# Decay differences in a chunked state-space scan: from mask products on TensorE to broadcast rows of running sums

## What is computed

```python
acum = jnp.cumsum(dt * a_neg.reshape(G, R), axis=2)
seg = acum[:, :, :, None] - acum[:, :, None, :]
decay = jnp.exp(jnp.where(causal[:, :, None, None], seg, -jnp.inf))
cb = jnp.einsum('bclgn,bcsgn->bclsg', Cm, Bm)
wts = cb[..., None] * decay * dt[:, :, None]
y_diag = jnp.einsum('bclsgr,bcsgrp->bclgrp', wts, x)
```

## Time and profile before

| | |
|---|---|
| median of the runs | 1535.14 us (1532.01 to 1537.67) |
| the profiled execution, its own time | 1531.77 us |
| its span in the trace | 1530.0 us |
| granted TensorE clock, mean | 0.949 of full |
| TensorE busy | 1419.6 us, 93% of the span |
| VectorE busy | 554.8 us, 36% |
| ScalarE busy | 389.2 us, 25% |
| POOL busy | 441.1 us, 29% |

### The profile page before, as it was taken

The page is one execution under the profiler, slowest core; times in us unless marked ns, Lnnn a source line. Parts: engine busy times, 40 slices in busy tenths (PEclk is TensorE's granted clock), DMA queues, the critical chain, the costliest instruction groups (busy, mean ns, idle before and its releaser), DMA issues.

```text
span 1530.0 us, 24111 instructions
## 1 busy us (share of the span) xinstructions
PE 1419.6 (93%) x9214; PEld 1217.3 (80%) x9214; DVE 554.8 (36%) x798; ACT 389.2 (25%) x581; POOL 441.1 (29%) x382
## 2 busy tenths in 40 slices
PE   6999999999998999999899799999789999999990
PEld 6999999997687769768876799954778788878870
DVE  3344420055457547546653511111521111111115
ACT  5211134443234234233323411101211101111112
POOL 5244433344235324433532433300010100010002
PEclk8999999999999989999999899999689999999995
DMA  5233222252044025106203222366149999999925
GB/s 135 56 82 76 77 70 78 82 139 56 1 135 105 14 64 148 42 0 161 78 14 89 56 82 74 118 226 284 47 155 341 344 327 344 344 337 337 343 91 199
DMA packets 179226, 220.04 MB, mean 144 GB/s; under 512 B 9193, under 2 KB 150633, under 8 KB 170943
## 3 DMA queue, kind: packets, MB, share of 16 engines
q1 hardware_dynamic: 166666, 183.20, 37.7%
q0 software_dynamic: 5040, 17.83, 3.8%
q10 hardware_dynamic: 7486, 18.56, 3.3%
HBM read 192.27 MB, written 27.30 MB: 144 GB/s over the span
## 4 chain that ended last, share of the span: by engine, by line
PE 77%; DVE 11%; issue 4%; DMA 3%; ACT 2%; SPq 1%; POOL 1%; DVEq 1%; ACTq 0%; POOLq 0%
PE acc L521 34%; PE pT L800 8%; PE pS L800 7%; PE acc L730 4%; PE acc L807 4%; DVE area L978 4%; PE pS L615 2%; PE pY L807 2%; PE acc L792 2%; PE pO L647 2%; PE pY L658 2%; PE pO L807 2%; DVE big L1049 1%; DMA ring<-in_w_in 1%; SPq L427 1%
## 5 line engine op out<-in xcount | busy, mean ns | idle before, releaser
L521 PE MATMUL acc<-h_parts,ring_parts 128*128 128x328 f32 (+1 forms) x3840 | 552.9, 305 | 5.0 <-POOL ring_parts L1528 4.3
L521 PEld LDWEIGHTS acc<-h_parts,ring_parts 128*128 128x128 f32 x3840 | 537.0, 191 | 21.1 <-issue 20.4
L1528 POOL TENSOR_TENSOR ring_parts<-ring,ring_parts 128x1024 fp32r<-128x1024 f32 x104 | 261.8, 2517 | 427.6 <-ACT ring_parts L1294 427.6
L1294 ACT ACTIVATE ring_parts<-ring 128x1024 fp32r<-128x1024 f32 x104 | 110.1, 1058 | 371.8 <-PE acc L521 344.0
L800 PEld LDWEIGHTS pT<-big,area 128*128 128x128 f32 x1024 | 118.8, 195 | 8.8 <-issue 7.6
L800 PE MATMUL pT<-big,area 128*128 128x96 f32 x1024 | 118.6, 277 | 0.9 <-ACT big L1464 0.9
L521 PE MATMUL acc<-u_parts,ring_parts 128*128 128x264 f32 (+1 forms) x640 | 110.0, 300 | 0.0
L521 PE MATMUL acc<-area_parts,ring_parts 128*128 128x264 f32 (+1 forms) x512 | 92.7, 302 | 10.8 <-DVE u_parts L1058 10.8
L521 PEld LDWEIGHTS acc<-u_parts,ring_parts 128*128 128x128 f32 x640 | 97.1, 189 | 0.0
L978 DVE SCALAR_TENSOR_TENSOR area<-area,xvec 128x616 f32<-128x616 f32 x72 | 90.1, 1252 | 10.5 <-DVE area L976 0.6
L1676 POOL COPY idx<-ids 96x1 int32 x32 | 5.7, 180 | 304.7 <-PE acc L792 304.7
(11 more groups left out here) (302 smaller groups left out, 1641.6 us busy)
## 6 DMA issues: line engine op xcount, KB each, us to landing
ring<-in_w_in SPq DMA_DIRECT2D x80, 512.0 KB, 4.0
area<-in_w_gate SPq DMA_DIRECT2D x24, 1024.0 KB, 5.7
area<-in_w_up SPq DMA_DIRECT2D x24, 1024.0 KB, 8.8
area<-in_w_down SPq DMA_DIRECT2D x24, 1024.0 KB, 11.0
y_first<-big ACTq DMA_DIRECT2D x32, 384.0 KB, 8.0
area<-in_state_ssm SPq DMA_DIRECT2D x16, 512.0 KB, 6.9
out<-area SPq DMA_DIRECT2D x16, 512.0 KB, 6.2
ring<-in_w_ssd_out SPq DMA_DIRECT2D x16, 512.0 KB, 3.8
```

The costliest lines, as they stand in the source:

```text
L521: m = nc.tensor.matmul(acc[a][:, h, 0:n], w[s][:, k, :], x[:, k, h * HALF:h * HALF + n], start=first and k == 0 and w is w_hi and x is hi, ...
L1294: a_.activation(w_hi[b % 2], w_raw[b % 2], ACT.Copy).then_inc(hi_done, 1)
L1528: gp.tensor_tensor(w_lo[b % 2], w_raw[b % 2], w_hi[b % 2].bitcast(F32), ALU.subtract).then_inc(lo_done, 1)
```

## The change

The running sums of each tile, for all 32 heads, are made in both layouts. As columns they are copied from `pY` over `da`, now called `acum`. As rows they come from five further products (`da` as weights, `m_le` moving), which ScalarE copies to SBUF and stores to HBM as `acum_rows`, one transfer for each tile. In tile i ScalarE itself loads the rows of the group's 8 heads, broadcast over all partitions, straight into `wts` (`load_row`); `wts` has now two buffers of 8 heads, by the parity of the tile. Rows 0 and 1 are loaded at the start of a group, row i + 1 in tile i for i = 1 to 3. POOL subtracts: acum[s] - row[l] in place. ScalarE applies Relu to the difference, then the exponential of its negative. VectorE multiplies all 8 heads with `cbm` in one instruction. The products of line 615, `rbuf` and the semaphore `p_seg` are gone. POOL's order around the tiles is changed: `split_lo` of blocks 8 and 9 comes before the subtractions for tiles 2 and 3. POOL's step at line 1623 now waits for the Y products of tile 3 and for ScalarE's copy of line 1383, not for the mask products of tile 4. A few semaphores of a path for overfull experts are shared with other ones, since their number is limited.

```diff
@@ TensorE, once @@
+                rows = pT[0:HEADS, i * P:i * P + r] if i < 4 else pS[0:HEADS, HEADS:HEADS + r]
+                nc.tensor.matmul(rows, d_i, le[0:r, 0:r], start=True, stop=True)
@@ TensorE, tile i @@
-                    for q in range(2):
-                        if q == 1 and i < 3:
-                            pe_block(pe, g_block(g, 7 + i), 7 + i, hT_hi, hT_lo, part=0)
-                        pe.wait_ge(s_r, g * 10 + (2 * i + q + 1))
-                        pe.wait_ge(s_exp, g * 10 + (2 * i + q + 1))
-                        if q == 0:
-                            pe.wait_ge(s_st, g * 6 + (i + 1))
-                        nc.tensor.matmul(pS[0:r, 0:4 * r], gt[0:r, 0:r], rbuf[0:r, q, 0:4 * r],
-                                         start=True, stop=True).then_inc(p_seg, 1)
-
+                    if i < 3:
+                        pe_block(pe, g_block(g, 7 + i), 7 + i, hT_hi, hT_lo, part=0)
+                    pe.wait_ge(s_st, g * 6 + (i + 1))
@@ VectorE, tile i @@
-                    for q in range(2):
-                        dve.wait_ge(s_exp, g * 10 + (2 * i + q + 2))
-                        w = wts[0:r, q, 0:4 * r].rearrange("p (h c) -> p h c", h=4)
-                        v.tensor_tensor(w, w, cbm[0:r, 0:r].unsqueeze(1).broadcast_to([r, 4, r]), ALU.mult
-                                        ).then_inc(s_w, 1)
+                    dve.wait_ge(s_exp, g * 5 + (i + 1))
+                    w = wts[0:r, i % 2, 0:HPG * r].rearrange("p (h c) -> p h c", h=HPG)
+                    v.tensor_tensor(w, w, cbm[0:r, 0:r].unsqueeze(1).broadcast_to([r, HPG, r]), ALU.mult).then_inc(s_w, 1)
@@ ScalarE, once @@
+            a_.activation(acum[:, :, :], pY[:, 0:160].rearrange(f3, h=HEADS), ACT.Copy)
+            a_.activation(acum_t[0:HEADS, 0:4 * P], pT[0:HEADS, :], ACT.Copy)
+            a_.activation(acum_t[0:HEADS, 4 * P:T], pS[0:HEADS, HEADS:HEADS + R4], ACT.Copy).then_inc(s_dta, 1)
+            act.wait_ge(s_dta, 8)
+            for i in range(TILES):
+                dst = acum_rows[0, HEADS * P * i:HEADS * (P * i + ROWS[i])].rearrange("(h l) -> h l", h=HEADS)
+                act.dma_start(dst, acum_t[0:HEADS, tok(i)]).then_inc(acum_out, 16)
@@ ScalarE, start of a group @@
+                def load_row(i):
+
+                    r = ROWS[i]
+                    act.wait_ge(p_y, g * 5 + (1 if i == 0 else i))
+                    if i == 1:
+                        act.wait_ge(s_rm, g + 1)
+                    src = acum_rows[:, bass.ds(g * (HPG * r) + HEADS * P * i, HPG * r)]
+                    act.dma_start(wts[0:r, i % 2, 0:HPG * r], src.broadcast_to([r, HPG * r])).then_inc(row_of[i % 2], 16)
+
+                load_row(0)
+                load_row(1)
@@ ScalarE, tile i, after the copy of line 1383 @@
-                    act.wait_ge(p_y, g * 5 + (i + 1))
-                    for q in range(2):
-                        act.wait_ge(p_seg, g * 10 + (2 * i + q + 3))
-                        a_.activation(wts[0:r, q, 0:4 * r], pS[0:r, 0:4 * r], ACT.Exp).then_inc(s_exp, 1)
+                    if 1 <= i <= 3:
+                        load_row(i + 1)
+                    act.wait_ge(s_r, g * 5 + (i + 1))
+                    w = wts[0:r, i % 2, 0:HPG * r]
+                    a_.activation(w, w, ACT.Relu).then_inc(s_neg, 1)
+                    act.wait_ge(s_neg, g * 5 + (i + 1))
+                    a_.activation(w, w, ACT.Exp, scale=-1.0).then_inc(s_exp, 1)
@@ POOL, the group's tiles @@
-                def decays(i, q):
+                def decays(i):
...
+                    hold(pool, row_of[i % 2], g * per_group + first)
+                    w = wts[0:r, i % 2, 0:HPG * r].rearrange("p (h c) -> p h c", h=HPG)
+                    gp.tensor_tensor(w, acum[0:r, i, bass.ds(g * HPG, HPG)].unsqueeze(2).broadcast_to([r, HPG, r]), w,
+                                     ALU.subtract).then_inc(s_r, 1)
+
+                decays(0)
                 split_lo(g_block(g, 6), 6)
...
+                decays(1)
+                split_lo(g_block(g, 7), 7)
...
+                split_lo(g_block(g, 8), 8)
+                decays(2)
+                split_lo(g_block(g, 9), 9)
+                decays(3)
+                decays(4)
 
                 hold(pool, s_bt, g * 5 + 5)
-                hold(pool, p_seg, g * 10 + 12)
+                hold(pool, p_y, g * 5 + 5)
```

More of the change, by code:

```diff
@@ L87, in build @@
         sdec = sb("sdec", [R4, HEADS])
+        acum = da
         dg = sb("dg", [P, GK, 2])
@@ L165, in build @@
         sg, _ = carve(0, [3, T])
+        acum_t, _ = carve(4 * T, [T])
         WE = 3 * 2048
@@ L219, in build @@
         wexp = [expert_slot(u) for u in range(UNROLL)]
+        acum_rows = nc.dram_tensor("acum_rows", [1, HEADS * T], F32).ap()
         h2_rows = nc.dram_tensor("h2_rows", [T, D], F32).ap()
@@ L251, in build @@
         s_hist, s_tail, s_cvd, s_silu = (sem(n) for n in ("s_hist", "s_tail", "s_cvd", "s_silu"))
-        p_xt, p_cb, p_seg, p_yo, p_y, p_sn, p_yt = (sem(n) for n in ("p_xt", "p_cb", "p_seg", "p_yo", "p_y", "p_sn", "p_yt"))
+        p_xt, p_cb, p_yo, p_y, p_sn, p_yt = (sem(n) for n in ("p_xt", "p_cb", "p_yo", "p_y", "p_sn", "p_yt"))
+        acum_out, s_neg = sem("acum_out"), sem("s_neg")
+        row_of = [sem("row_of0"), sem("row_of1")]
         s_u, s_y1, s_y2, s_xd, s_cb, s_bt, s_r, s_exp, s_w, s_st = (
@@ L279, in build @@
         f_back, f_add = sem("f_back"), sem("f_add")
-        f_w, f_id, f_cast, f_x, f_tr, f_xe, f_gu, f_silu, f_act, f_dn, f_ye, f_out, f_skip = (
-            sem(n) for n in ("f_w", "f_id", "f_cast", "f_x", "f_tr", "f_xe", "f_gu", "f_silu", "f_act", "f_dn", "f_ye",
-                             "f_out", "f_skip"))
+        f_w, f_id, f_cast, f_x, f_dn, f_out, f_skip = (
+            sem(n) for n in ("f_w", "f_id", "f_cast", "f_x", "f_dn", "f_out", "f_skip"))
         g_in = [sem(f"g_in{i}") for i in range(TILES)]
@@ L316, in hs_tiles, with row_loads @@
                     (slice(64, R4), slice(6, 8), last[:, 0:256]))
+        def row_loads(i):
+            return 48 if i % 2 == 0 else 32, 16 * (i // 2 + 1)
         def conv_tile(turn, c):
@@ L598, in _ @@
                     r = ROWS[i]
-                    le, gt = (m_le, m_gt) if i < 4 else (m_le4, m_gt4)
                     for k in range(GK):
@@ L837, in _ @@
                         pe.wait_ge(f_x, n * 16 + 16)
-                        to_rows(0, f_tr)
+                        to_rows(0, m_tr)
                         pe.wait_ge(f_w, n * 48 + 48)
-                        pe.wait_ge(f_xe, n + 1)
-                        gate_up(0, 0, pT, f_gu)
-                        pe.wait_ge(f_act, n + 1)
+                        pe.wait_ge(m_xe, n + (NE + 2))
+                        gate_up(0, 0, pT, m_gu)
+                        pe.wait_ge(m_act, n + (NE + 1))
                         down(0, 0, down_banks[0], f_dn)
@@ L1345, in _ @@
             split_hi(g_block(0, 0), 0)
+            act.wait_ge(acum_out, 16 * TILES)
             with act.Fori(0, GROUPS) as g:
@@ L1606, in _ @@
-                decays(0, 0)
-                decays(0, 1)
-                split_lo(g_block(g, 6), 6)
-                for i in range(1, TILES):
-                    for q in range(2):
-                        decays(i, q)
-                    if i < 4:
-                        split_lo(g_block(g, 6 + i), 6 + i)
-                    if i == 1:
-                        hold(pool, s_silu, g * 6 + 8)
-                        gp.tensor_copy(cmask[:, 0:LASTP], cT[:, 4 * P:TP])
-                        diag = cmask[:, R4 + LASTP:R4 + LASTP + NSEQ * (R4 + SLEN)].rearrange("p (s c) -> p s c", c=R4 + SLEN)
-                        gp.tensor_copy(diag[:, :, 0:SLEN], cT[:, TP:T].rearrange("p (s c) -> p s c", c=SLEN)).then_inc(s_cm, 1)
+                    per_group, first = row_loads(i)
```

36 lines of the change are left out of this document (15 added, 21 removed).

## The result

The changed kernel takes 1548.88 us (median of 4 runs, 1547.77 to 1552.38), the kernel before in the same session 1535.59 us. The ratio is 1.0088, with a 95% interval of 1.0069 to 1.0108: 13 us slower, where 4 us faster was forecast, with a range that ended at 1542.

What follows compares the result with a forecast made beforehand. TensorE was taken to bound the kernel (77% of the chain). Four groups of -3.1 us gave -12.2, +1.1 once, +6.8 clock: -4.3, so 1527.5 from the profiled 1531.8, or 1530.8 from the median 1535.1; range 1519 to 1542.

Steps and rivals of the forecast that it cites:

- Tiles 0 to 2: Two mask products leave TensorE's gapless row: period 13.1 to 11.4 us, gain 5.2 us per group.
- Tile 3's chain: POOL, ScalarE and VectorE steps put tile 3's Y product 9.15 us after block 9, was 8.36: 0.8 us lost per group.
- meeting (a): POOL's subtraction for tile 4 meets VectorE's product of tile 3 in SBUF: 0 to 1.2 us per group, taken 0.4.
- Meeting (b): POOL's mask step (line 1623), now earlier, meets VectorE's copy at line 997 in tile 4: 0 to 0.6 us, taken 0.6.
- Meeting (c): Ahead of tile 0, POOL's one longer subtraction meets VectorE's last convolution steps: 0 to 0.6 us per group, taken 0.3.
- The rows: Twenty broadcast transfers of up to 512 KB, issued by ScalarE, land before they are needed: cost nothing.
- D: Rival: the rows land late, at 13.3 us, costing 5.3 us per group, 21 in all: 1552 us; chance 0.07.
- E: Rival: Relu and Exp don't share a function table; loads of 1.28 us add 11.5 in all: 1542.3 us; chance 0.05.
- Once: Five products transposing the running sums, 0.22 us each, add 1.1 us on TensorE; ScalarE's copies and stores cost nothing.
- The clock: TensorE's thin stretch around tile 3 brings half clock: 0 to 3.4 us per group, taken 1.7, 6.8 in all.
- B: Rival: the clock stays up, -11.1 us, 1524.0; without POOL and VectorE meeting either, -16.3, 1518.8; chance 0.27.
- C: Rival: POOL and VectorE hold each other fully and clock costs 3.4 us per group: +6.9 in all, 1542; chance 0.10.

Runs made afterwards that it cites:

- e1_fill_gap: Kernel after the change, plus idle TensorE products after tile 3's transposes, ahead of its Y products and after tile 4's transposes; 1529.3 us, ratio 0.9948.
- e7_all: Kernel after the change, with POOL's old order, the mask step late, and idle products in tiles 3 and 4 and ahead of tile 0; 1509.4 us, ratio 0.9839.
- e9_before_filled: Kernel before the change, plus idle products ahead of tile 0, between the mask products of tiles 3 and 4, and ahead of tile 3's Y products; 1527.2 us.
- e2_before_fill_front: Kernel before the change, plus four pairs of idle products in TensorE's gap ahead of tile 0; 1528.0 us, ratio 0.9960.
- e10_before_gap: Kernel before the change, with five scratch products on VectorE in tile 3 that delay its Y products; 1557.5 us, ratio 1.0148.
- e11_before_gap_filled: Kernel before the change, with the same five scratch VectorE products in tile 3 and idle TensorE products in the gap; 1547.6 us, ratio 1.0075.

## Why the prediction was wrong, by its own steps

**Tiles 0 to 2: right.** 11.4 us periods, forecast 11.4. In tile 0 part of it went to the clock (below): from its first transposes to those of tile 1 it is 13.0 us in group 0, 0.1 less than before.

**Tile 3's chain: right.** Forecast 9.2 us after block 9, and 9.6 with the 0.4 of meeting (a); measured 9.53. The timeline answers to the earlier trace rows, step by step:

```profile
530.49 1.06 ACT L1290 ACTIVATE ring_parts<-ring 128x1024 fp32r<-128x1024 f32 x1 [3.76 <-PE acc L528]
...
531.62 2.36 POOL L1546 TENSOR_TENSOR ring_parts<-ring,ring_parts 128x1024 fp32r<-128x1024 f32 x1 [7.08 <-ACT ring_parts L1290]
...
533.94 1.90 POOL L1620 TENSOR_TENSOR area<-da,area 128x1024 f32<-128x1024 f32 x1
...
535.87 1.06 ACT L1403 ACTIVATE area<-area 128x1024 f32<-128x1024 f32 x1 [1.10 <-POOL area L1620]
...
536.96 1.06 ACT L1405 ACTIVATE area<-area 128x1024 f32<-128x1024 f32 x1
537.54 1.25 POOL L1620 TENSOR_TENSOR area<-da,area 80x640 f32<-80x640 f32 x1 [1.71 <-DMA area<-acum_rows]
538.12 1.76 DVE L1007 TENSOR_TENSOR area<-area 128x1024 f32<-128x1024 f32 x1 [1.77 <-ACT area L1405]
```

VectorE's product takes 1.76 us instead of 1.23, since POOL's subtraction for tile 4 began 0.6 us earlier: meeting (a), 0.5 us, where 0.4 was taken. POOL's step had 0.67 us left when the product began, and the product took 0.53 longer. Here the trace agrees with the page "SBUF — State Buffer" of the Trainium skill (Who interferes with whom) that the later one waits for the end of the earlier. In the four groups the product takes 1.60, 1.76, 1.78 and 1.69 us, so 0.4 to 0.55 us were lost and in no group the full 1.2.

**Meeting (b): right in kind, a little small.** Line 996 takes 1.32 us beside POOL's step that begins at 547.81; 0.9 us lost in group 1 where 0.6 was the upper bound. In groups 0 to 3 the line takes 1.08, 1.32, 1.73 and 1.25 us, the longer the sooner it begins behind POOL's step (1.11, 0.87, 0.46 and 0.94 us); with the full clock in tiles 3 and 4 (e1_fill_gap) it is 1.08 in all four, 0.67 lost.

```profile
547.81 1.91 POOL L1640 TENSOR_TENSOR area<-area,m_blk 80x1024 f32<-80x1024 f32 x1 [9.02 <-ACT area L1398]
...
548.68 1.32 DVE L996 COPY area<-sdec 80x512 f32 x1
```

**Meeting (c): right.** The three convolution steps take 4.44 us instead of 4.13.

**The rows: right, nothing.** They land in a median of 3.9 us, and ScalarE loads a table at line 1405 four times in all, once a group, as at line 1387 before. Rivals D and E are out, and e7_all, which has all the rows, leaves no room for them.

```profile
area<-acum_rows ACTq DMA_DIRECT2D x16, 512.0 KB, 3.9
```

**Once: 2.1 us, not 1.1.** From the first product with `da` to the next projection block it is 5.5 us, and was 3.5. The new products stand 0.34 us apart from their followers, not 0.22. After this longer thin stretch the granted clock is at half for 3.4 to 6.8 us in seven of the nine traces that have the new products, though not in that of the kernel after, and in one of the five that don't have them.

**The clock: the step that failed.** The mechanism was named, the size was wrong. I took one stretch of 3.4 us at half clock per group, 1.7 us, and 3.4 as the bound. Filling the gaps of tiles 3 and 4 gives back 19.6 us, 4.9 per group (e1_fill_gap against after). Three things were missing in the estimate. The clock didn't come back after one stretch: in group 1 it stayed down for 10.2 us, in which TensorE did small products and transposes and waited for VectorE. Then it fell again in tile 4, where it had fallen in two of four groups before. And in tile 0 it lasted longer (group 1) or came where it had not been (group 0). The bound of 3.4 us was a guess at "twice", not a bound: I read how long one low stretch had lasted in two places, and used it in a place where thin work (small products with waits between them) follows for 15 us. The trace of the kernel before already had longer ones: nine low stretches begin within its loop, four of 3.4 us and five of 6.8. One of the long ones is at the start of tile 0 of group 3, behind the same 3.8 us without work (the first two of these lines):

```profile
750.50:753.90 3.40, 2.63 (x10) 2.12 (x10) 1.37 (x3) 3.02 (x7) 1.74 (x1) 0.51 0.00 0
753.90:757.30 3.40, 3.40 (x14) 2.88 (x14) 1.29 (x2) 1.34 (x2) 1.66 (x2) 0.50 0.47 106
757.30:760.70 3.40, 3.40 (x19) 2.44 (x18) 0.28 (x1) 0.60 (x1) 0.69 (x1) 0.99 0.16 49
```

With the measured terms the sum of a group is -5.2 for tiles 0 to 2, +1.1 for the start of tile 3's Y products, +0.9 and +0.3 for meetings (b) and (c), and +4.9 for the clock: +2.0, so +8.0 for four, and +10 with 2.1 once. Measured were +13. Of the 3 us left, 1.8 stand in tiles 0 to 2, whose stretch from the first transposes to the Y products of tile 2 became 18.9 us shorter over the four groups instead of 20.6, for the half clock in tile 0.

**The rivals.** B, without the clock, gave -11.1; e1_fill_gap is at -6.7 and, with less half clock left in both kernels, e7_all is 16 to 18 us under e9_before_filled, near the -16.3 of B without the meetings (in e7_all the mask step's meeting is out, and tile 3's chain is shorter as well). The lower end of the working was sound. C had the right mechanisms and ended at +7, with the clock at two thirds of what was measured; the range ended there too.

**What stays open.** Before the loop the two profiled executions differ by 2.3 us in the first 40 us, which no edit touches. The clock is at half there from 23.5 to 44.0 us before the change and from 21.0 to 48.3 after it; over all fourteen profiled kernels this first stretch is 20.5, 23.9 or 27.3 us long, each of them with and without the change, so it is not put down to it. The spans of the profiled executions differ by 17 us and the medians by 13, since the profiled execution of the kernel before lay 3.8 us under its median. That the longer low clock in tile 0 comes from the changed spacing and not from chance was not tested; e2_before_fill_front and e7_all show only that idle products take it away. Relu was not taken off the chain; what it costs there was not tried.

## What to carry to other kernels

Work taken off the busiest engine is a gain only where that engine has no gap next to it; where another chain ends last, the removal makes a gap, and on TensorE the gap can lower the granted clock for the dense or thin work behind it. So price a gap by its length plus what TensorE's work loses until the clock is back, look in the trace for the longest low stretch and not for the first, and try idle products in the gap before giving up a change: here they turned +0.9% into -0.5%, and with POOL's old order, the later mask step and idle products ahead of tile 0 into -1.6%. Before moving one engine's step behind another's handshake (here POOL's subtraction behind the split of a weight block), follow the new chain to the first consumer without cover.

## What the runs showed of the hardware

- Idle products of ones into an unused accumulator held the granted clock at 1.00 through tiles 3 and 4, and held up the Y products by some 0.1 us in two groups and not at all in the other two (e1_fill_gap); 3.4 us of them ahead of tile 0 did the same (e2_before_fill_front).
- The Y products, sixteen records of 64 columns, take 1.9 us at the full clock and 3.65 at half; they are short in columns, but take the full factor.
- The gap of e10_before_gap, 3.8 us in an otherwise unchanged kernel, cost about 10 us over four groups beyond its length, against the same delay with the gap filled (e11_before_gap_filled).
- VectorE's copy of 80x512 with one operand in SBUF stands still while POOL works (0.41 us alone, 1.08 to 1.73 beside it), as VectorE's products of two SBUF operands do (0.69 and 1.18 us; 1.23 and 1.76).
